# A two-block transformer kernel: the experts' gather by pairs in two bursts, and a first norm by a diagonal matrix

## The chip, the cores and the metric

The kernel runs on one core of one Trainium2 chip. The metric is the device time of one execution in microseconds. It is a single program of some 28,000 instructions on the engines TensorE (PE in the profile, its weight loads PEld), VectorE (DVE), ScalarE (ACT), GpSimd (POOL) and SyncE (SP, which here only issues transfers).

## The reference

The input x is 256 tokens of 1024 float32 values. Two blocks follow each other, and all arithmetic is float32. The chain is:

- a norm, a short convolution mixer, a norm, a dense SwiGLU (2816 wide);
- a norm, latent attention, a norm, a mixture of 8 experts (each a SwiGLU 2048 wide, two of them per token);
- SwiGLU, block attention, SwiGLU, SwiGLU, a state-space mixer (Mamba 2), SwiGLU, each with its norm.

Two parts matter here:

```python
def rmsnorm(x, g):
    xf = x.astype(jnp.float32)
    y = xf * lax.rsqrt(jnp.mean(xf * xf, axis=-1, keepdims=True) + EPS)
    return (y * g.astype(jnp.float32)).astype(x.dtype)

def moe_swiglu(h, router, w_gate, w_up, w_down):
    ...
    vals, idx = lax.top_k(probs, TOP_K)
    wts = vals / jnp.sum(vals, axis=-1, keepdims=True)
    ...
    for e in range(N_EXPERTS):
        out = out + gates[:, e:e + 1] * swiglu(ht, w_gate[e], w_up[e], w_down[e])
```

## The kernel before, in words

**Weights.** All large weights lie in HBM as slabs of 128 x 2048 float32 (1 MB). SP loads them in order into six buffers (`raw`); a load of slab s + 6 waits until slab s is split. ACT rounds a slab to the float32r format (`whi`, line 642, in `split_hi`), and DVE takes the rest (`wlo = raw - whi`, line 1142). There are three buffers for each of the two (`SPLIT`), so ACT begins slab n only when TensorE has used slab n - 3. Each product is three: hi by hi, hi by lo and lo by hi (`three`, lines 1874 to 1876, and `cols_slab`, lines 1949 to 1951). Activations are held as hi and lo parts in the same way.

**Order of work.** Every engine has one instruction stream in program order, and semaphores order them against each other. The code of each engine goes slab by slab: at slab k it first splits slab k + 2 (`ahead`) and then does what else stands at k.

**A norm that isn't deferred** is the first one and the one ahead of the state-space mixer. ACT squares and sums the two token tiles (`squares`, line 655), POOL computes the root (`root`, lines 515 and 517), DVE scales both tiles of x into `hn` (`scaled`, line 1170), and TensorE transposes `hn` in four banks' worth (`norm_T`, line 1901), with two buffers (`tp`) in turn. ACT (`norm_hi`, line 662) and DVE (`norm_lo`, line 1154) make the operand's hi and lo parts, multiplied by the gain, which is a column of `vecs`. Before the second of these norms TensorE runs 24 products with zeros (`idle_products`, line 1881), whose results nobody reads.

**The start.** Eleven small DMAs on ACT's queue load the gain and convolution vectors as rows into `vec_rows` (line 1082). TensorE runs 26 idle products, transposes the three row tiles (line 2578), DVE copies them to `vecs` (line 1803), and TensorE runs ten more idle products. SP waits for x before it issues the first slab.

**The experts** (`routed`). Where no expert has over 128 tokens, each expert's rows are gathered. Per expert there are 24 slabs in eight chunks of three: `up_a`, `up_b` (gate and up projections, k half by half) and `down`. After `up_b` come ACT's silu (line 745) and DVE's product (`h_tok`, line 1513); after `down` come TensorE's transposes of h_tok for the next chunk (line 2388), then `hT_hi` on ACT (line 752) and `hT_lo` on DVE (line 1517). `each_expert` writes out expert 0 and expert 7 and loops three times over a pair of an odd and an even one.

An expert's gather multiplies the token rows (`rows_hi`, `rows_lo`) by a 0/1 matrix `pick` of 256 tokens by 128 places. DVE makes `pick` (`choose`, line 1477) at slab 12; TensorE gathers after slab 14 in 32 products (line 2365) into two accumulator banks; ACT (line 728) and DVE (line 1486) convert the result to `xg_hi` and `xg_lo`, two of eight parts per slab, ACT at slabs 15 to 18 and DVE at 17 to 20. `pick` is transposed to `put` for the way back: ACT and DVE make `yg_hi` (line 735) and `yg_lo` (line 1495) at slab 2 of the next expert, TensorE scatters after slabs 3 and 5 (lines 2371 and 2372), and DVE adds to x at slabs 4 and 6 (line 1501). Ahead of expert 0 stand 22 idle products, its gather, and 12 idle products.

```python
                    if not last and k == OPERAND_AT - 1:
                        if not first:
                            pe.wait_ge(x_ready, f.x0 + 2 * ex)
                        gather(ex + 1, ex + 1)
```

Of the kernel before, what the change touches and what calls it, by code (L numbers as in the profile page):

```python
# [25 lines left out]
P = 128  # L26
# [25 lines left out]
OPERAND_AT = 15  # L52
# [5 lines left out]
def program(nc, a, out):  # L58
    ctx = ExitStack()
    with ctx:  # L60
# [67 lines left out]
        rows_loaded = sem("rows_loaded")  # L128
        rows_zero = sem("rows_zero")
        vecs_full = sem("vecs_full")  # L130
# [21 lines left out]
        def col(v, n):  # L152
            return vecs[:, v[0], v[1] + n:v[1] + n + 1]

        row_loads = [(V_MIX, 16, a["norm_mix"]), (V_FFN, 16, a["norm_ffn"]), (V_CONV, 24, a["conv_w"]),
                     (V_QA, 3, a["mla_q_a_norm"]), (V_KVA, 2, a["mla_kv_a_norm"]), (V_FFN1, 16, a["ffn1_norm_2"]),
                     (V_MIX2, 16, a["mix_norm_2"]), (V_FFN2, 16, a["ffn2_norm_2"]), (V_SCONV, 128, a["ssm_conv_w_2"]),
                     (V_SBIAS, 32, a["ssm_conv_b_2"]), (V_SNORM, 16, a["ssm_norm_2"])]

# [32 lines left out]
        vec_rows = big[:, 6144:6144 + 3 * P].rearrange("p (a b) -> p a b", a=3)  # L192
# [138 lines left out]

        rt = [area(8192 + 16 * n, 16).rearrange("p (t e) -> p t e", t=NT) for n in range(8)]
# [16 lines left out]
        pick = hT_hi[:, 2 * P:4 * P]  # L349
        put = big_r[:, 2 * D:2 * D + NT * P]  # L350
# [4 lines left out]
        yg_hi_done = sem("yg_hi_done")  # L355
        iota_i = area(8832, P).bitcast(I32)
# [99 lines left out]
        def each_expert(e, fn):  # L456

            def body(ex, first, last, parity):
                for k in range(0 if first else 2, 3 * (F_EXPERT // FC) + (0 if last else 2)):
                    fn(k, ex, first, last, parity)  # L460

            body(0, True, False, 0)
            with e.Fori(0, EXPERTS // 2 - 1) as i:
                body(2 * i + 1, False, False, 1)
                body(2 * i + 2, False, False, 0)
            body(EXPERTS - 1, False, True, 1)
# [12 lines left out]
        def _(sp):  # L479
# [16 lines left out]
            sp.wait_ge(x_loaded, 16 * NT)  # L496
# [138 lines left out]
        def _(act):  # L635
# [12 lines left out]
            def squares(f):  # L648
# [5 lines left out]
                for t in range(NT):  # L654
                    act.activation(hn[:, t], x[:, t], ACT.Square, accum_out=n_sum[:, f.m, t:t + 1]).then_inc(norm_sum, 1)

            def norm_hi(f, bs):
                v, g0 = f.gain
                for b in bs:
                    act.wait_ge(tp_full, f.u0 + b + 1)  # L660
                    for j in range(2):
                        r = act.activation(actA_hi[:, 2 * b + j, :], tp[:, (f.u0 + b) % 2, j * SEQ:(j + 1) * SEQ],
# [15 lines left out]
            def norm(f):  # L678
                if f.m == 0:
                    act.wait_ge(vecs_ready, 1)  # L680
# [39 lines left out]
            def routed(f):  # L720
# [3 lines left out]
                def operand(e, kt, parity):  # L724

                    if kt == 0:
# [1990 lines left out]
```

## Time and profile before

| | |
|---|---|
| time, median of 3 runs | 2200.74 us (2199.27 to 2201.12) |
| time of the profiled execution | 2198.36 us |
| its span in the profile | 2196.6 us |
| TensorE clock granted, mean | 0.989 |
| read from HBM | 454.77 MB, 208 GB/s over the span |

The experts take the stretch from about 450 to 1058 us of the span. In a timeline each row gives the start, the duration of the merged instructions, and in brackets the engine's idle time before them with what released it. A TensorE product's own duration is longer than the distance to the next one, because products overlap: the distance of the starts counts.

### The profile page before, as it was taken

How to read it: one execution, taken by the hardware profiler on the slowest of the kernel's cores; microseconds unless marked ns; L12 is line 12 of the kernel's file. 1: busy time of each engine (PE TensorE's matmuls, PEld its weight loads, DVE VectorE, ACT ScalarE, POOL GpSimd, SP SyncE). 2: the span in 40 equal slices, each digit the busy share in tenths (PEclk: the TensorE clock that was granted, in tenths of full speed). 3: DMA queues.
4: the chain of work that ended last, by engine and by line, in shares of the span. 5: the costliest groups of instructions: out<-in, count | busy, mean ns of one | idle time of the engine just before them, and what ended most of it. 6: DMA issues, size and time to landing. Idle time of an engine off the chain costs nothing.

```text
span 2196.6 us, 28406 instructions
## 1 busy us (share of the span) xinstructions
PE 2125.2 (97%) x10573; PEld 1777.1 (81%) x10573; DVE 1426.5 (65%) x1510; ACT 1182.0 (54%) x1361; POOL 56.6 (3%) x102
## 2 busy tenths in 40 slices
PE   9999998789999999999899999999999999989999
PEld 8888886578887888888788777888788799878887
DVE  5654556458889889889555585545555488585554
ACT  4444456357767777777444465444444466555433
POOL 1000001000000000000100010000000000000000
PEclk9999999989999999999999999999999999999999
DMA  8555433248898889889555443555455345314551
GB/s 278 182 182 191 166 141 115 78 180 339 329 360 326 344 326 357 328 344 355 183 186 191 158 168 125 199 184 185 172 187 191 138 154 193 133 41 180 185 188 57
DMA packets 64584, 457.07 MB, mean 208 GB/s; under 512 B 7457, under 2 KB 7950, under 8 KB 9838
## 3 DMA queue, kind: packets, MB, share of 16 engines
q1 hardware_dynamic: 63616, 455.24, 56.1%
q0 software_dynamic: 448, 0.46, 0.3%
q8 instruction: 59, 0.97, 0.2%
q14 instruction: 31, 0.25, 0.0%
q10 hardware_dynamic: 430, 0.15, 0.0%
HBM read 454.77 MB, written 1.05 MB: 208 GB/s over the span
## 4 chain that ended last, share of the span: by engine, by line
issue 63%; PE 30%; DVE 3%; POOL 1%; DVEq 1%; ACT 1%; ACTq 0%; POOLq 0%; DMA 0%
PE gu L1874 4%; PE gu L1876 4%; PE gu L1875 4%; PE acc L1874 3%; PE acc L1875 3%; PE acc L1876 3%; PE acc L1949 2%; PE acc L1951 2%; PE acc L1950 2%; DVE wlo L1142 1%; PE tp L1963 0%; PE tp L1901 0%; DVEq L1696 0%; POOL qk_rstd L612 0%; DVE big L1697 0%
## 5 line engine op out<-in xcount | busy, mean ns | idle before, releaser
L1142 DVE TENSOR_TENSOR wlo<-raw,whi 128x2048 fp32r<-128x2048 f32 (+1 forms) x436 | 989.5, 2271 | 417.1 <-ACT whi L642 415.9
L642 ACT ACTIVATE whi<-raw 128x2048 fp32r<-128x2048 f32 (+1 forms) x436 | 827.1, 1898 | 237.7 <-PE acc L1876 190.1
L1874 PE MATMUL gu<-whi,actA_hi 128*128 128x512 f32 (+1 forms) x1456 | 578.8, 398 | 2.7 <-DVE actA_lo L1154 1.8
L1876 PE MATMUL gu<-whi,actA_lo 128*128 128x512 f32 (+1 forms) x1456 | 567.7, 390 | 0.0
L1875 PE MATMUL gu<-wlo,actA_hi 128*128 128x512 f32 (+1 forms) x1456 | 566.4, 389 | 0.0
L1876 PEld LDWEIGHTS gu<-whi,actA_lo 128*128 128x128 f32 x1456 | 273.5, 188 | 58.5
L1874 PEld LDWEIGHTS gu<-whi,actA_hi 128*128 128x128 f32 x1456 | 274.0, 188 | 57.0 <-issue 3.9
L1875 PEld LDWEIGHTS gu<-wlo,actA_hi 128*128 128x128 f32 x1456 | 274.4, 188 | 53.0
L1874 PE MATMUL acc<-whi,hT_hi 128*128 128x512 f32 x656 | 257.3, 392 | 2.1 <-DVE hT_lo L1517 2.1
L1876 PE MATMUL acc<-whi,hT_lo 128*128 128x512 f32 x656 | 256.3, 391 | 0.0
L1875 PE MATMUL acc<-wlo,hT_hi 128*128 128x512 f32 x656 | 256.0, 390 | 0.0
L1874 PEld LDWEIGHTS acc<-whi,hT_hi 128*128 128x128 f32 x656 | 123.6, 188 | 30.8 <-DVE wlo L1142 2.6
L1876 PEld LDWEIGHTS acc<-whi,hT_lo 128*128 128x128 f32 x656 | 123.5, 188 | 26.0
L1875 PEld LDWEIGHTS acc<-wlo,hT_hi 128*128 128x128 f32 x656 | 123.6, 188 | 25.3
L695 ACT ACTIVATE hT_hi<-tp 128x512 fp32r<-128x512 f32 x50 | 29.9, 598 | 200.3 <-PE tp L1963 200.3
L1949 PE MATMUL acc<-actA_hi,whi 128*128 128x256 f32 x448 | 127.6, 285 | 0.8 <-DVE wlo L1142 0.8
L1951 PE MATMUL acc<-actA_hi,wlo 128*128 128x256 f32 x448 | 126.7, 283 | 0.0
L1950 PE MATMUL acc<-actA_lo,whi 128*128 128x256 f32 x448 | 126.7, 283 | 0.0
L1193 DVE TENSOR_TENSOR hT_lo<-tp,hT_hi 128x512 fp32r<-128x512 f32 x50 | 34.6, 692 | 115.6 <-ACT hT_hi L695 115.6
L1874 PE MATMUL acc<-whi,actA_hi 128*128 128x512 f32 (+1 forms) x224 | 89.1, 398 | 2.7 <-DVE actA_lo L1744 1.9
L710 ACT ACTIVATE silu_g<-gu,n_rstd 128x256 f32<-128x256 f32 x55 | 26.1, 475 | 119.3 <-PE gu L1876 119.3
L1949 PEld LDWEIGHTS acc<-actA_hi,whi 128*128 128x128 f32 x448 | 85.9, 192 | 1.1 <-DVE wlo L1142 1.1
(387 smaller groups left out, 2227.3 us busy)
## 6 DMA issues: line engine op xcount, KB each, us to landing
raw<-in_slabs SPq DMA_DIRECT2D x427, 1024.0 KB, 4.8
raw<-in_slabs SPq DMA_DIRECT2D x4, 576.0 KB, 3.8
raw<-in_slabs SPq DMA_DIRECT2D x2, 768.0 KB, 4.2
raw<-in_slabs SPq DMA_DIRECT2D x2, 640.0 KB, 3.9
x<-in_x SPq DMA_DIRECT2D x2, 512.0 KB, 3.8
out<-x SPq DMA_DIRECT2D x2, 512.0 KB, 2.8
raw<-in_slabs SPq DMA_DIRECT2D x1, 128.0 KB, 2.3
aux<-in_mla_q_norm POOLq DMA_DIRECT2D x1, 96.0 KB, 6.7
```

The costliest lines, as they stand in the source:

```text
L642: act.activation(whi[:, n0 % SPLIT, 0:w], raw[:, n0 % RAW, 0:w], ACT.Copy).then_inc(slab_hi, 1)
L695: act.activation(to[0], tp[:, (f.u0 + c) % 2], ACT.Copy).then_inc(tp_hi, 1)
L710: act.activation(silu_g[:, 1, :], gu[:, 1, 0:FC], ACT.Silu, scale=n_rstd[:, f.m - 1, 1:2]).then_inc(gu_silu, 1)
L1142: dve.tensor_tensor(wlo[:, n0 % SPLIT, 0:w], raw[:, n0 % RAW, 0:w], whi[:, n0 % SPLIT, 0:w].bitcast(F32), ALU.subtract).then_inc(slab_spli ...
L1193: dve.tensor_tensor(to[1], tp[:, (f.u0 + c) % 2], to[0].bitcast(F32), ALU.subtract).then_inc(tp_read, 1)
L1874: pe.matmul(o, xh, wh, start=start, stop=False)
L1875: pe.matmul(o, xh, wl, start=False, stop=False)
L1876: return pe.matmul(o, xl, wh, start=False, stop=stop)
L1949: pe.matmul(o, w[0][:, kt, bs], aT_hi[:, kt], start=kt == 0, stop=False)
L1950: pe.matmul(o, w[0][:, kt, bs], aT_lo[:, kt], start=False, stop=False)
L1951: r = pe.matmul(o, w[1][:, kt, bs], aT_hi[:, kt], start=False, stop=kt == KT - 1)
```

## The change

**The first norm and the one ahead of the state-space mixer.** ACT squares the first tile, DVE the second. POOL's root is as before. DVE then multiplies the identity by the root of each token (`rstd_diag`, two tiles of 128 x 128), and TensorE multiplies x by that diagonal matrix, which transposes and scales in one product, in float32. The very first norm uses four banks (two of them in `gu`) and doesn't wait for them to be read. The second of these norms has 18 idle products for 24.

**The vectors.** The host lays them out as columns, and one DMA on ACT's queue loads `vecs`. The row loads, the three transposes, the copy and ten of the idle products go; of the first 26 there remain 22. ACT runs a one-tile Square on zeros before it waits for x. SP issues slabs without a wait for x. On DVE slab 0's lo part now stands between the norm's first two banks and the last two.

**The experts.** Gathers are made for pairs (2q, 2q + 1). `pick` holds two experts' places side by side, in `hT_hi` for the first token tile and in `hT_lo` for the second. In an odd expert's slabs DVE chooses at slab 7; TensorE gathers half of the features after slab 8 and the other half after slab 15, with 16 products of 256 columns each, into the same two banks; ACT converts the even expert's part to `xg_hi` and copies the odd one's to `xg_odd` in float32, two of each per slab at 9 to 12 and 16 to 19; DVE makes the even expert's lo part, one of eight per slab, at 11 to 14 and 18 to 21. In an even expert ACT makes the odd one's `xg_hi` of `xg_odd` in one instruction at slab 12, and DVE its lo part at slab 13. The gather ahead of expert 0 is for the pair and uses four banks. `put` has two buffers, one per parity, and is made in chunk 1, not 3.

```diff
-OPERAND_AT = 15
+GATHER_AT = (8, 15)
+ODD_AT = 12
@@ norm, any engine
+        def norm_bank(f, b):
+            return gu[:, b - 2] if f.m == 0 and b >= 2 else tp[:, (f.u0 + b) % 2]
@@ SP
-            sp.wait_ge(x_loaded, 16 * NT)
@@ ACT, squares
-                for t in range(NT):
+                for t in range(NT if f.deferred else 1):
@@ ACT, routed
-                def operand(e, kt, parity):
-                    if kt == 0:
-                        act.wait_ge(gathered, e + 1)
-                    r = act.activation(xg_hi[parity][...], acc[:, 2 + kt // 4, ...], ACT.Copy, scale=col(v, g0 + kt))
+                def operand(q, kt, odd, base=2):
+                    if kt % 4 == 0 and not odd:
+                        act.wait_ge(gathered, 2 * q + kt // 4 + 1)
+                    o = xg_odd if odd else xg_hi[0]
+                    r = act.activation(o[:, kt * P:(kt + 1) * P], acc[in_pair(kt, odd, base)], ACT.Copy, scale=col(v, g0 + kt))
+                    if kt % 2 and odd:
                         r.then_inc(xg_hi_done, 1)
+                def odd_operand():
+                    act.drain()
+                    act.activation(xg_hi[1], xg_odd, ACT.Copy).then_inc(odd_hi_done, 1)
-                    if not last and OPERAND_AT <= k < OPERAND_AT + KT // 2:
-                        for j in range(2):
-                            operand(ex + 1, 2 * (k - OPERAND_AT) + j, 1 - parity)
+                    odd, q = pair
+                    if odd and not last:
+                        for n in range(2):
+                            if GATHER_AT[n] < k <= GATHER_AT[n] + 4:
+                                for j in range(2):
+                                    operand(q + 1, 4 * n + k - GATHER_AT[n] - 1, j)
+                    if not odd and k == ODD_AT:
+                        odd_operand()
@@ ACT, start
-            act.wait_ge(rows_zero, 1)
-            for v, n, src in row_loads:
-                ...
-                act.dma_start(vec_rows[...], ...).then_inc(rows_loaded, 16)
+            act.dma_start(vecs[:, :, :].rearrange("p a b -> p (a b)"), a["vecs"]).then_inc(vecs_ready, 16)
+            act.wait_ge(zero_ready, 1)
+            act.activation(area(2400, P), zero_r[:, :].bitcast(F32), ACT.Square)
@@ DVE, norm
-            def scaled(f):
-                dve.wait_ge(norm_rstd, f.m + 1)
-                for t in range(NT):
-                    dve.tensor_scalar(hn[:, t], x[:, t], n_rstd[:, f.m, t:t + 1], None, ALU.mult).then_inc(norm_tok, 1)
+            def diagonal(f):
+                if f.x0 == 0:
+                    dve.wait_ge(x_loaded, 16 * NT)
+                dve.drain()
+                dve.scalar_tensor_tensor(hn[:, 1], x[:, 1], 1.0, x[:, 1], ALU.mult, ALU.mult,
+                                         accum_out=n_sum[:, f.m, 1:2]).then_inc(norm_sum, 1)
+                dve.wait_ge(masks_ready, 2)
+                dve.wait_ge(norm_rstd, f.m + 1)
+                for t in range(NT):
+                    r = dve.tensor_scalar(rstd_diag[:, t], ident[:, :], n_rstd[:, f.m, t:t + 1], None, ALU.mult)
+                r.then_inc(norm_tok, 1)
@@ DVE, routed
+                        for odd in range(2):
+                            r = dve.tensor_scalar(pick[t][:, odd * P:(odd + 1) * P], iota, slot_of[:, at_expert(t, 2 * q + odd)],
+                                                  None, ALU.is_equal)
+                def odd_operand(q):
+                    dve.wait_ge(odd_hi_done, q + 1)
+                    dve.tensor_tensor(xg_lo[1], xg_odd, xg_hi[1].bitcast(F32), ALU.subtract).then_inc(odd_lo_done, 1)
-                    if not last and k == 12:
-                        choose(ex + 1)
+                    if odd and not last:
+                        if k == GATHER_AT[0] - 1:
+                            choose(q + 1)
+                        for n in range(2):
+                            if GATHER_AT[n] + 2 < k <= GATHER_AT[n] + 6:
+                                operand(q + 1, 4 * n + k - GATHER_AT[n] - 3)
+                    if not odd and k == ODD_AT + 1:
+                        odd_operand(q)
@@ DVE, start
-            dve.memset(vec_rows[:, :, :], 0.0).then_inc(rows_zero, 1)
-                scaled(stages_used[0])
-            dve.wait_ge(vecs_full, 1)
-            dve.tensor_copy(vecs[...], gu[:, 1, 0:3 * P]).then_inc(vecs_ready, 1)
-            ahead(0, -2)
-            norm(stages_used[0])
+                diagonal(stages_used[0])
+            norm_lo(stages_used[0], (0, 1))
+            ahead(0, -2)
+            norm_lo(stages_used[0], (2, 3))
@@ PE, norm
-                    if u >= 2:
+                    if u >= 2 and f.m:
                         pe.wait_ge(tp_read, u - 1)
-                            idle_products(gu[:, 0], 24)
-                        pe.wait_ge(norm_tok, 2 * (f.dm + 1))
+                            idle_products(gu[:, 0], 18)
+                        pe.wait_ge(norm_tok, f.dm + 1)
+                            if f.deferred:
+                                r = pe.transpose(o, part, ident[:, :])
+                            else:
+                                r = pe.matmul(o, part, rstd_diag[:, t], start=True, stop=True)
@@ PE, routed
-                def gather(e, n):
-                    pe.wait_ge(picked, n + 1)
-                    for kt in range(KT):
+                def gather(q, n, base=2):
+                    if n == 0:
+                        pe.wait_ge(picked, q + 1)
+                    elif base == 2:
+                        pe.wait_ge(xg_lo_done, 2 * q + 1)
+                    for kt in range(4 * n, 4 * n + 4):
-                    if kind == "up_a" and c % C == 0:
-                        pe.wait_ge(xg_lo_done, ex + 1 + c // C)
+                    if kind == "up_a" and c == C:
+                        if odd:
+                            pe.wait_ge(xg_lo_done, 2 * q + 4)
+                        else:
+                            pe.wait_ge(odd_lo_done, q + 1)
-                    if not last and k == OPERAND_AT - 1:
-                        if not first:
-                            pe.wait_ge(x_ready, f.x0 + 2 * ex)
-                        gather(ex + 1, ex + 1)
+                    if odd and not last and k in GATHER_AT:
+                        if k == GATHER_AT[0]:
+                            pe.wait_ge(x_ready, f.x0 + 2 * ex)
+                        gather(q + 1, GATHER_AT.index(k))
                 gather(0, 0)
+                gather(0, 1, 0)
@@ PE, start
-            idle_products(gu[:, 0], 26)
+            idle_products(gu[:, 0], 22)
             pe.wait_ge(masks_ready, 2)
-            pe.wait_ge(rows_loaded, 16 * len(row_loads))
-            for t in range(3):
-                r = pe.transpose(gu[:, 1, t * P:(t + 1) * P], vec_rows[:, t, :], ident[:, :])
-            r.then_inc(vecs_full, 1)
-            idle_products(gu[:, 0], 10)
-            pe.wait_ge(vecs_ready, 1)
```

## Rows read from the trace of the kernel before

**Rows 1.** The page, busy time of each engine over the span.

```profile
PE 2125.2 (97%) x10573; PEld 1777.1 (81%) x10573; DVE 1426.5 (65%) x1510; ACT 1182.0 (54%) x1361; POOL 56.6 (3%) x102
```

**Rows 2.** Windows in the experts: length, busy PE, PEld, DVE, ACT, POOL, clock, DMA, GB/s.

```profile
593.00:663.00 70.00, 69.73 (x329) 57.00 (x329) 61.79 (x51) 49.47 (x47) 0.00 (x0) 1.00 0.92 352
```

**Rows 3.** Waits from 457.4 to 1058 us: total, times, longest.

```profile
PEld tp L2388 <- DVE h_tok L1513: 8.1, 15, 2.8
```

**Rows 4.** Timeline of TensorE, transposes of h_tok in the second and third expert.

```profile
558.21 0.38 PE L2388 MATMUL tp<-ident,h_tok 128*128 128x128 f32 x2
...
566.63 0.38 PE L2388 MATMUL tp<-ident,h_tok 128*128 128x128 f32 x2
...
575.28 0.38 PE L2388 MATMUL tp<-ident,h_tok 128*128 128x128 f32 x2
...
587.34 0.38 PE L2388 MATMUL tp<-ident,h_tok 128*128 128x128 f32 x2
...
595.89 0.44 PE L2388 MATMUL tp<-ident,h_tok 128*128 128x128 f32 x2
...
604.71 0.44 PE L2388 MATMUL tp<-ident,h_tok 128*128 128x128 f32 x2
...
649.46 0.38 PE L2388 MATMUL tp<-ident,h_tok 128*128 128x128 f32 x2
```

**Rows 5.** Timeline of the start, 0 to 27 us, all engines.

```profile
1.12 7.86 PE L1881 MATMUL gu<-zero_r 128*128 128x512 f32 x26 [1.12 <-DVE zero_r L1135]
...
5.46 37.67 SPq L483 DMA_DIRECT2D raw<-in_slabs  x12
...
6.49 1.28 ACT L655 ACT_TABLE_LOAD   x1 [6.49 <-issue]
...
10.40 0.72 POOL L517 TENSOR_TENSOR n_rstd<-n_ms,n_half 128x2 f32<-128x2 f32 x1
...
12.95 2.28 DVE L1142 TENSOR_TENSOR wlo<-raw,whi 128x2048 fp32r<-128x2048 f32 x1
...
15.61 1.04 PE L1901 MATMUL tp<-ident,big 128*128 128x128 f32 x8
...
19.31 0.36 PE L1949 MATMUL acc<-actA_hi,whi 128*128 128x256 f32 x1
...
22.26 0.28 PE L1949 MATMUL acc<-actA_hi,whi 128*128 128x256 f32 x1
```

**Rows 6.** Windows of the start, columns as in rows 2.

```profile
3.00:4.00 1.00, 1.00 (x4) 0.81 (x3) 0.00 (x0) 0.00 (x0) 0.00 (x0) 1.00 1.01 406
...
12.20:14.00 1.80, 1.80 (x5) 1.36 (x5) 1.80 (x3) 0.18 (x1) 1.80 (x4) 0.50 1.02 432
```

**Rows 7.** Timeline of DVE in the second expert.

```profile
560.19 0.42 DVE L1517 TENSOR_TENSOR hT_lo<-tp,hT_hi 128x256 fp32r<-128x256 f32 x1
...
574.53 0.47 DVE L1477 TENSOR_SCALAR hT_hi<-big 128x128 fp32r<-128x128 f32 x2
```

**Rows 8.** Timeline of ACT in the second expert.

```profile
572.81 0.39 ACT L745 ACTIVATE silu_g<-gu 128x256 f32<-128x256 f32 x1 [0.86 <-PE gu L1876]
573.10 1.92 ACT L642 ACTIVATE whi<-raw 128x2048 fp32r<-128x2048 f32 x1
```

**Rows 9.** Timeline of the norm ahead of the state-space mixer.

```profile
1745.66 1.04 ACT L655 ACTIVATE big<-x 128x1024 f32<-128x1024 f32 x1
...
1747.96 1.50 DVE L1170 TENSOR_SCALAR big<-x,n_rstd 128x1024 f32<-128x1024 f32 x2 [3.38 <-POOL n_rstd L517]
...
1749.51 1.09 PE L1901 MATMUL tp<-ident,big 128*128 128x128 f32 x8 [0.82 <-DVE big L1170]
```

**Rows 10.** Timeline of TensorE in the state-space mixer.

```profile
1902.02 1.05 PE L2518 MATMUL acc<-h_tok 128*128 128x128 f32 x8
...
1905.38 0.65 PE L2533 MATMUL gu<-aux 128*128 128x256 f32 x2
```

**Rows 11.** Groups by line, the gathers' products with rows_lo.

```profile
L2365 PE MATMUL acc<-hT_hi,actB_lo 128*128 128x128 f32 x128 | 29.0, 276 | 0.0
```

More of the change, by code:

```diff
@@ L348, in program @@
         yg_hi, yg_lo = [big_r[:, D * n:D * n + D] for n in range(2)]
-        pick = hT_hi[:, 2 * P:4 * P]
-        put = big_r[:, 2 * D:2 * D + NT * P]
+        pick = [v[:, 2 * P:4 * P] for v in (hT_hi, hT_lo)]
+        xg_odd = area(3072, D)
+        put = [big_r[:, 2 * D + NT * P * n:2 * D + NT * P * (n + 1)] for n in range(2)]
         route_const, route_sel, route_cum, route_flag, rows_hi_done, rows_lo_done = [sem(n) for n in (
@@ L749, in at @@
                         bank = tp[:, (f.u0 + t) % 2]
-                        if t == 3:
-                            act.activation(put, bank[:, 2 * P:4 * P], ACT.Copy)
+                        if t == 1:
+                            act.activation(put[pair[0]], bank[:, 2 * P:4 * P], ACT.Copy)
                         act.activation(hT_hi[:, 0:2 * P], bank[:, 0:2 * P], ACT.Copy).then_inc(tp_hi, 1)
-                    if not last and OPERAND_AT <= k < OPERAND_AT + KT // 2:
-                        for j in range(2):
-                            operand(ex + 1, 2 * (k - OPERAND_AT) + j, 1 - parity)
+                    odd, q = pair
[6 more added lines that the diff above has]
+                        odd_operand()
                 for kt in range(KT):
-                    operand(0, kt, 0)
+                    for j in range(2):
+                        operand(0, kt, j, (2, 0)[kt // 4])
                 each_expert(act, at)
@@ L1502, in add, with at @@
                                              x[:, t], ALU.mult, ALU.add).then_inc(x_ready, 1)
-                def at(k, ex, first, last, parity):
+                def at(k, ex, first, last, pair):
                     kind, c = ffn_kind(f, k, ex)
@@ L1518, in at @@
                                           ALU.subtract).then_inc(tp_read, 1)
-                    if not last and k == 12:
-                        choose(ex + 1)
-                    if not last and OPERAND_AT + 2 <= k < OPERAND_AT + 2 + KT // 2:
-                        for j in range(2):
-                            operand(ex + 1, 2 * (k - OPERAND_AT - 2) + j, 1 - parity)
+                    odd, q = pair
+                    if odd and not last:
[6 more added lines that the diff above has]
+                        odd_operand(q)
                 choose(0)
                 for kt in range(KT):
-                    operand(0, kt, 0)
+                    operand(0, kt, (2, 0)[kt // 4])
                 each_expert(dve, at)
@@ L2706 @@
     weights = slabs({k: np.asarray(v) for k, v in inputs.items() if k in PACKED})
[L2707 to L2708 removed]
+    plain = {k: v for k, v in inputs.items() if k not in PACKED | COLUMNS}
+    for name, value in {**plain, "slabs": weights, "vecs": columns(inputs), **constants()}.items():
         v = np.ascontiguousarray(value)
```

109 lines of the change are left out of this document (54 added, 55 removed).

## The prediction

> **What bounds the kernel now.** I read the page first: TensorE is busy for 97% of the span [rows 1], so only what shortens TensorE's own queue, or a wait in front of it, can move the time. Then the experts' stretch by windows: in a typical 70 us PE is busy for 69.7, DVE for 61.8, ACT for 49.5, and the DMA engines carry 352 GB/s at a 0.92 share [rows 2]. PE sets the pace; DVE has little left. Then the waits of that stretch, of which the transposes' wait for DVE's h_tok, 8.1 us in 15 times, is one of TensorE's longest [rows 3]; no engine waits there for a weight transfer. Last the timeline of the transposes, which come once per three slabs and so act as a ruler [rows 4]: 558.21 to 566.63 is 8.42 us for three slabs with nothing between; the next gap is 8.65 (two transposes of `pick` in it); the one with the gather is 12.06; the two after it are 8.55 and 8.82, for DVE then has two operand conversions at each slab. A gather in the loop so costs 3.64 + 0.13 + 0.40 = 4.17 us. Seven of the eight gathers are in the loop: **29.2 us**. From 8.42, with some 0.25 for the transposes, a slab is 2.72.
>
> **The first norm.** Before, ACT issues eleven DMAs and reaches its table load at 6.49; squares, root and scaling follow; n_rstd is ready at 11.12, ten idle products stand before the transposes at 15.61, slab 0 is split at 15.23, and its first matmul runs at 19.31 [rows 5]. After, one DMA replaces the eleven on ACT's queue, the table load moves in front of the wait for x, SP doesn't wait for x (its first slab was issued at 5.46) and DVE takes one of the squares. In order: 0.2 MB of vectors beside x at 406 GB/s [rows 6] puts x at 5.9 for 5.4; squares to 7.2 (DVE's is unseen; the split's 2.28 for 2048 elements makes it about half of that, 1.15 to 1.3); POOL's root 1.1 (0.72 is the power) to 8.35; two diagonals of 128 columns, 0.47 as the picks of [rows 7], to 8.85. The 22 idle products (26 took 7.86) end by 8.1 and cost nothing. Sixteen products into four banks end near 10.8. Meanwhile slab 0 follows x and the vectors: 5.9 + 1.05 MB at 406 GB/s = 8.5. ACT: whi, 1.92 by [rows 8], to 10.4, then eight norm_hi of 0.39, as that group's other row, to 13.6; DVE: norm_lo of two banks, 0.42 each half as in [rows 7], to 12.9, wlo of slab 0 to 15.2. That is the new start, 4.0 us earlier. But PE now stands idle from 10.8 to 15.2, and before, idle from 8.98 on was followed by a granted clock of 0.50, the 1.2 GHz level, in 12.2 to 14.0 [rows 6]. If the low clock holds for twice that stretch, the 256-column products of slab 0 take some 0.21 instead of 0.12 each (24 in 2.95 us, [rows 5]): 1.6 lost. I take **2.4**, between 0.5 (vectors and slabs delay x by two more) and 4.2 (the clock stays up). Slab 1 is split near 19.2, before slab 0 is used up. POOL's own DMAs stay behind its root and only come earlier. Four banks save the waits for tp_read, but DVE is what ends last here.
>
> **The norm before the state-space mixer.** ACT's second square (1.04 at 1745.66) goes to DVE beside the first, where it ends 0.2 later; two scalings (1.50 at 1747.96) become two diagonals of 0.47. So the transposes now at 1749.51 come 1.04 - 0.2 + 1.03 = 1.9 earlier [rows 9]. Six idle products fewer are 6 x 2.72 / 12 = 1.4; PE stood idle for 0.82 in front of the transposes, so 0.3 of that is left and nothing is held up. What follows (hi, lo, two banks) moves along. The products with the diagonal are true f32 matmuls. Such a product of 128 columns has a pitch of (1.05 - 0.27) / 7 = 0.11 us, one of 256 columns about 0.24 [rows 10], and the present transposes have 0.11 too (eight in 1.04, [rows 5]): no price. I take **1.8**, between 0.5 (the clock falls in another place) and 2.2. The Trainium skill (TensorE: Matmul & The Clock Gate, Terms) says that transpose mode is 4x faster for FP32, so that leaving it should cost; at 128 columns this trace disagrees, and what the rule would make of the time is the third rival's.
>
> **The experts.** Each gather of today is 32 products of 128 columns ([rows 11]: 128 of the half rows_lo, as many of the other), 3.64 us in the ruler, 0.114 each. A pair's gather is 32 products of 256 columns, 0.123 each by slab 0 [rows 5], 3.9 us, in two bursts: twice the columns cost nearly the same. The gather ahead of the loop grows by 0.3 and has sixteen conversions on ACT for eight, in the shadow of twelve idle products; if that cover were short it is 0.3 to 0.5 once. In the loop three pair gathers, 11.7, replace 29.2: at most 17.5 saved. New waits:
> - The choice is of four, 0.94, twice the 0.47 of [rows 7], and stands at slab 7, one slab before the burst. In the body shown, DVE's hT_lo starts at 560.19, so the picks are ready at 561.5; slab 8 ends at 566.63 - 2 x 2.72 = 561.2. PE waits **0.4**, and behind it stand the burst's results and slab 9; DVE's next split is 0.6 late, for which the burst itself makes room. Three times.
> - DVE's operand conversions are one per slab over eight slabs, not two over four, with a burst before each four: **0.2** for today's 0.53.
> - The odd half of a pair: in each even expert ACT copies 128x1024 at slab 12 and DVE subtracts at 13. Read against the body shown: silu at 572.81, whi of slab 15 at 573.10 for 1.92 [rows 8]. With a copy (half a whi, 1.0) between them whi ends at 576.0 and wlo at 578.25, just when PE needs it (575.28 + 0.25 + 2.72). hT_lo and the subtraction (1.15, half a split) put wlo of slab 16 at 579.75 to 582.0, and PE wants it at 581.0: **1.0** late, four times.
> So 3 x (3.9 + 0.4 + 0.2) + 4 x 1.0 = 17.5 stands against 29.2: **11.7** saved. Ends: 17.5 (no new wait) and 7.4 (waits of 1.5 a pair, copies 1.2 each: 16.2 + 5.6 with the conversions' own). The transposes of `pick` stay two per expert; the scatter is untouched.
>
> **The sum.** 2.4 + 1.8 + 11.7 = 15.9. The profiled execution took 2198.36 us, which gives 2182.5; the median of the runs shown, 2200.74, is 2.4 above it, and against that the forecast is **2184.8**.
>
> **Rivals.**
> 1. The odd copies and picks hide after all, and PE pays for little but the products. For it: DVE's adds of 128x1024 at slabs 4 and 6 leave no mark on the ruler at 566.63. Against: there the scatter gives PE other work. Experts 17.0, sum 21.2: 2179.5. Chance 0.14.
> 2. More conflict, the lower end: 7.4 + 4.2 = 11.6: 2189.1. Chance 0.08.
> 3. Products with the diagonal run at four times the transposes' pitch, 0.44. The second bank of the first norm is then full at 12.4, slab 0 is split at 16.3 (1.1 lost), and the later norm, whose four banks cost 1.3 more each, partly side by side, loses 3.5: 2189.4. This is what the skill's sentence on transpose mode would make. Against it stands the 0.11 of [rows 10]. Chance 0.05.
> 4. Transfers bind the experts. 575.28 to 649.46 is one expert [rows 4], 24 slabs of 1.05 MB in 74.2 us, 339 GB/s. If 340 were the most, the experts would gain nothing: sum 4.2, about 2196. Against: no wait for raw, and 352 in [rows 2], where the forecast asks for 346. Chance 0.06.
> 5. **Slower.** DVE becomes the pace at the burst slabs: the choice, the lo halves that the second burst waits for, and the odd subtraction each come behind a split that went first, one slab late. Ten places (3 + 3 + 4). Without new waits the sum is 21.7; above 2.2 us a place the change loses, above 2.6 it loses more than can be mistaken, and at a whole slab, 2.72, the time is 2206. For: DVE 61.8 of 70. Against: two conversions per slab cost 0.53 in all. Chance 0.03.
> That the experts take the all-token branch, so that the change is void there, is excluded for this input by the products of [rows 11].
>
> **The numbers.** Forecast 0.64, rivals 0.14, 0.08, 0.05, 0.06, 0.03. The range joins the bounds of the terms: 0.5 + 0.5 + 7.4 = 8.4 to 4.2 + 2.2 + 17.5 = 23.9 saved, 2176.8 to 2192.3; it leaves out rivals 4 and 5. What a measurement of this kernel can tell from no change is 0.2%, 4.4 us. Faster by more: all but rival 5 and half of rival 4, 0.94; within 0.2% 0.03; slower 0.03.
>
> **What would show it.** Start: n_rstd near 8.3, the first matmul of slab 0 near 15.2, with half-clock products after it; a start near 17 would mean that x or slab 0 came late. Later norm: transposes about 1.0 behind n_rstd's own end with a pitch of 0.11. Experts: the ruler should read 8.4 and 1.9 more in a gap with a burst, 0.4 more at the first; about 9.4 once in each even expert, where the odd half is subtracted; two experts that took 148.4 should take about 145.5. ACT waiting for raw, or gaps over 10.8 without a scatter, would prove me wrong.

## The result, and the profile after

| | before | after |
|---|---|---|
| median of the runs | 2200.01 us (4 runs) | 2182.36 us (4 runs) |
| lowest to highest | 2197.30 to 2201.12 | 2180.46 to 2186.71 |
| profiled execution | 2198.36 | 2180.46 |
| its span | 2196.6 | 2178.7 |
| TensorE busy | 2125.2, 10573 instructions | 2104.8, 10454 |

The ratio is 0.9931, with an interval of 0.9915 to 0.9947: 15.2 us faster (11.7 to 18.7), where 15.9 was forecast. The two medians of the table lie 17.7 apart, inside the same interval. The two profiled spans differ by 17.9 us. TensorE stays the bound. This is the page's line of busy times after, to be set against [rows 1]:

```profile
PE 2104.8 (97%) x10454; PEld 1760.3 (81%) x10454; DVE 1422.8 (65%) x1484; ACT 1184.7 (54%) x1362; POOL 56.0 (3%) x102
```

TensorE is 20.4 us less busy, DVE and ACT are what they were. Five points of TensorE's timeline split the 17.9 us of the two spans:

| point | before | after | gained up to it |
|---|---|---|---|
| first product of slab 0 | 19.31 | 15.54 | 3.8 |
| first product of the gather ahead of expert 0 | 450.35 | 446.75 | 3.6 |
| last transposes in the experts | 1046.22 | 1030.46 | 15.8 |
| idle products ahead of the state-space mixer | 1743.09 | 1727.35 | 15.7 |
| first full-width product of that mixer | 1757.39 | 1739.55 | 17.8 |

So 3.6 us came at the start, 12.1 in the experts and 2.1 in the later norm. Nothing was given back between. Not all of it is the change's: at three of these places the profile of before has TensorE at a low clock where another execution of the same code has it high, and that is 1.7 us at the start, 1.6 at expert 0 and 1.3 in the later norm (experiment 2 and the hardware section). Without these 4.6 the 17.9 would be 13.3.

**The start.** The timeline of all engines after, 0 to 30 us, to be read against [rows 5]:

```profile
1.11 6.68 PE L1905 MATMUL gu<-zero_r 128*128 128x512 f32 x22 [1.11 <-DVE zero_r L1143]
...
1.24 1.28 ACT L1090 ACT_TABLE_LOAD   x1 [1.24 <-PEq L2749]
...
6.30 1.06 ACT L653 ACTIVATE big<-x 128x1024 f32<-128x1024 f32 x1 [3.45 <-DMA x<-in_x]
...
6.36 1.23 DVE L1180 SCALAR_TENSOR_TENSOR big<-x 128x1024 f32<-128x1024 f32 x1 [5.29 <-DMA x<-in_x]
...
8.02 0.71 POOL L515 TENSOR_TENSOR n_rstd<-n_ms,n_half 128x2 f32<-128x2 f32 x1
...
9.48 2.02 PE L1929 MATMUL tp<-silu_g,x 128*128 128x128 f32 x16 [1.68 <-DVE silu_g L1185]
...
11.34 1.95 PE L1929 MATMUL gu<-silu_g,x 128*128 128x128 f32 x16
...
13.20 2.28 DVE L1150 TENSOR_TENSOR wlo<-raw,whi 128x2048 fp32r<-128x2048 f32 x1
...
15.54 0.39 PE L1976 MATMUL acc<-actA_hi,whi 128*128 128x256 f32 x1 [2.25 <-DVE wlo L1150]
```

The table load lies in the wait for x, x is worked on at 6.30, and the root is ready at 8.73 (11.12 before). The last waits end in the order forecast: DVE's part of the split of slab 0 (`wlo`) releases TensorE. The two rows of line 1929 say something that the prediction had not read: two banks are eight products, and the row counts 16. A true float32 product of 128 columns leaves two records, where a transpose leaves one (eight per two banks in [rows 5]).

**The experts.** The ruler after, TensorE's transposes of h_tok, through most of an odd expert and all of the even one behind it ([rows 4] before):

```profile
540.74 0.38 PE L2418 MATMUL tp<-ident,h_tok 128*128 128x128 f32 x2
...
550.30 0.38 PE L2418 MATMUL tp<-ident,h_tok 128*128 128x128 f32 x2
...
561.00 0.38 PE L2418 MATMUL tp<-ident,h_tok 128*128 128x128 f32 x2
...
569.43 0.38 PE L2418 MATMUL tp<-ident,h_tok 128*128 128x128 f32 x2
...
579.86 0.38 PE L2418 MATMUL tp<-ident,h_tok 128*128 128x128 f32 x2
...
605.31 0.38 PE L2418 MATMUL tp<-ident,h_tok 128*128 128x128 f32 x2
...
615.19 0.38 PE L2418 MATMUL tp<-ident,h_tok 128*128 128x128 f32 x2
...
624.75 0.38 PE L2418 MATMUL tp<-ident,h_tok 128*128 128x128 f32 x2
...
641.58 0.38 PE L2418 MATMUL tp<-ident,h_tok 128*128 128x128 f32 x2
...
651.43 0.38 PE L2418 MATMUL tp<-ident,h_tok 128*128 128x128 f32 x2
```

A plain gap (561.00 to 569.43) is 8.43. The gaps of 9.88 and 9.56 hold the scatter, as in every expert, the second now with the transposes of `pick` too. What the change put in:

- 550.30 to 561.00, 10.70: the first burst, 1.92 for its 16 products and 0.36 of waiting.
- 569.43 to 579.86, 10.43: the second burst, 1.92 and 0.09.
- 641.58 to 651.43, 9.85: the odd half of a pair in an even expert, 1.43.

The waits of the stretch 440 to 1040 us (total, times, longest), against [rows 3]:

```profile
PEld tp L2418 <- DVE h_tok L1535: 2.8, 1, 2.8
...
PEld acc L2395 <- DVE hT_lo L1494: 1.5, 3, 0.5
```

TensorE waits once for h_tok, 15 times before. New are three waits of 0.5 for the picks, one ahead of each first burst.

The gap of 12.06 of [rows 4] is gone. From 540.74 one odd and one even expert take 146.1 us (the row one loop later is at 686.83); the prediction wanted 145.5 in place of 148.4.

### The profile page after: what moved, and what is told of

Same layout as the page of the kernel before. It is cut to its first block, busy times and chain, and to the rows that moved or that the text cites. A ratio compares the mean times of both kernels' runs of the same rounds, so it can differ in the third digit from the quotient of the medians.

```text
span 2178.7 us, 28140 instructions
## 1 busy us (share of the span) xinstructions
PE 2104.8 (97%) x10454; PEld 1760.3 (81%) x10454; DVE 1422.8 (65%) x1484; ACT 1184.7 (54%) x1362; POOL 56.0 (3%) x102
## 3 DMA queue, kind: packets, MB, share of 16 engines
HBM read 454.82 MB, written 1.05 MB: 209 GB/s over the span
## 4 chain that ended last, share of the span: by engine, by line
issue 63%; PE 30%; DVE 3%; POOL 1%; DVEq 1%; ACT 1%; DMA 0%; POOLq 0%; ACTq 0%; SPq 0%
PE gu L1898 4%; PE gu L1900 4%; PE gu L1899 4%; PE acc L1898 3%; PE acc L1899 3%; PE acc L1900 3%; PE acc L1976 2%; PE acc L1978 2%; PE acc L1977 2%; DVE wlo L1150 1%; PE tp L1990 0%; DVEq L1722 0%; POOL qk_rstd L610 0%; DMA raw<-in_slabs 0%; ACT whi L640 0%
```

## The experiments

The line numbers of kernel.py differ a little from kernel to kernel. All ratios are against the kernel before, which ran beside each.

**1. The norms alone.** The change's hunks of the start, the vectors and the two norms; the experts as before.

```diff
+            act.dma_start(vecs[:, :, :].rearrange("p a b -> p (a b)"), a["vecs"]).then_inc(vecs_ready, 16)
-                scaled(stages_used[0])
+                diagonal(stages_used[0])
...
```

> The change's norms and vectors alone, with the experts as before. If the parts add up, this saves what the trace of the changed kernel shows outside the experts: 3.8 us at the start and 2.1 us at the later norm, 5.9 us together, ratio 0.9973; slab 0's first product starts at 15.5 us, and the three-slab gaps of the experts read 12.05, 8.55 and 8.82 us after each gather as before. Rival: most of the start's gain is granted clock that another execution need not give; then slab 0's products have a pitch of 0.21 us in this run and the saving is 3 to 4 us.

Measured: 2195.68, ratio 0.9985 (0.9975 to 0.9994), 3.3 us and so less than expected (1.3 to 5.5 by the interval). Its profiled execution shows the same steps as the changed kernel: slab 0 begins at 15.67, the mixer's first full-width product stands 12.24 behind the idle products (14.30 before, 12.20 after), and its span, 2190.5, is 6.1 shorter. So the profiled execution gained what the pair of profiles said, and the median less. That made TensorE's clock suspect.

**2. The experts alone.** The change's hunks of `routed`; start and norms as before.

```diff
-                    if not last and k == OPERAND_AT - 1:
...
-                        gather(ex + 1, ex + 1)
+                    if odd and not last and k in GATHER_AT:
...
+                        gather(q + 1, GATHER_AT.index(k))
...
```

> The pair gather alone, with norms and vectors as before. The ruler of the changed kernel gives 29.4 us before and 13.4 (three pair gathers with their waits) plus 5.7 (four odd halves) after, so 10.3 us saved if expert 0's first three slabs run at the low clock as before, 11.9 if they do not: ratio 0.9953 or 0.9946. Rival (transfers or DVE give part of it back elsewhere in this stretch): under 8 us.

Measured: 2187.12, ratio 0.9947 (0.9931 to 0.9964), 11.7 us. The ruler takes 568.74 us from first to last transposes (580.67 before, 568.58 after); 1.6 of that difference is the clock at expert 0, whose first three slabs take 8.47 here and after, and 10.04 before. The parts add up, 3.3 + 11.7 = 15.0 against 15.2: the start is not paid for in the experts, nor the other way. This kernel has the start of before, instruction for instruction, and still begins slab 0 at 17.61, not 19.31. TensorE's timeline of it from 10 us:

```profile
11.52 2.56 PE L1908 MATMUL gu<-zero_r 128*128 128x512 f32 x10
...
17.61 0.36 PE L1976 MATMUL acc<-actA_hi,whi 128*128 128x256 f32 x1
```

Before, the same ten idle products took 4.00 at 11.77. The window 11.30 to 15.60 (columns as in [rows 2]) of before, and then of this kernel:

```profile
11.30:15.60 4.30, 4.24 (x13) 3.42 (x14) 3.93 (x4) 1.08 (x1) 4.30 (x7) 0.60 1.19 408
```

```profile
11.30:15.60 4.30, 3.65 (x21) 2.93 (x21) 4.03 (x5) 1.86 (x4) 4.30 (x7) 1.00 1.16 398
```

A granted clock of 0.60 against 1.00, with the same code ahead of it. The start of before is worth 19.3 in one execution and 17.6 in another, so of the 3.8 us that the start shows in the pair of profiles 1.7 depends on which execution of before was taken.

**3. The odd half in four pieces.** One copy and one subtraction of 128 x 1024 in an even expert become four of 128 x 256, two slabs apart.

```diff
-ODD_AT = 12
+ODD_AT = (9, 11, 13, 15)
-                    if not odd and k == ODD_AT + 1:
-                        odd_operand(q)
+                    if not odd and k - 1 in ODD_AT:
+                        odd_operand(q, ODD_AT.index(k - 1))
```

> The changed kernel, with the odd half made in four pieces of 256 columns: ACT at slabs 9, 11, 13, 15, DVE at 10, 12, 14, 16. If the 1.4 us that each even expert loses comes from two lumps in a row (a copy of 1.0 on ACT that makes slab 15's split late, a subtraction of 1.2 on DVE that makes slab 16's late), the 9.85 us gap falls to 8.5 and four of them save 5.3 us on the changed kernel. Rival: DVE as such lacks the time in this stretch, whatever the cut; then the loss spreads over other gaps and under 2 us is saved.

Measured: 2176.4, ratio 0.9905 (0.9886 to 0.9924). Its ruler in the same even expert:

```profile
643.07 0.38 PE L2422 MATMUL tp<-ident,h_tok 128*128 128x128 f32 x2
...
651.48 0.38 PE L2422 MATMUL tp<-ident,h_tok 128*128 128x128 f32 x2
```

The gap of 9.85 is 8.41. The odd half costs 1.4 us four times where it comes in one piece; the same work in four pieces costs nothing. (The cut and the slabs at which the work stands were changed together; a single piece was tried at one other slab only, in experiment 8.) The timeline of the changed kernel says who is late, ACT and DVE from 639 us:

```profile
639.57 1.06 ACT L734 ACTIVATE actA_hi<-big 128x1024 fp32r<-128x1024 f32 x1
...
640.54 1.90 ACT L640 ACTIVATE whi<-raw 128x2048 fp32r<-128x2048 f32 x1
...
642.47 2.29 DVE L1150 TENSOR_TENSOR wlo<-raw,whi 128x2048 fp32r<-128x2048 f32 x1 [1.56 <-ACT whi L640]
...
644.82 0.19 PEld L1898 LDWEIGHTS gu<-whi,actA_hi 128*128 128x128 f32 x1 [0.54 <-DVE wlo L1150]
...
645.01 1.21 DVE L1512 TENSOR_TENSOR actA_lo<-big,actA_hi 128x1024 fp32r<-128x1024 f32 x1
...
646.15 4.48 DVE L1150 TENSOR_TENSOR wlo<-raw,whi 128x2048 fp32r<-128x2048 f32 x2
...
648.56 0.49 PE L1898 MATMUL acc<-whi,hT_hi 128*128 128x512 f32 x1 [0.72 <-DVE wlo L1150]
```

ACT's copy holds back `whi` by 1.06; DVE waits 1.56 for it, and its `wlo` reaches TensorE 0.5 late. Then DVE's 1.21 makes the next `wlo` late by the rest, some 0.9. The prediction had the second of these and called the first just in time.

**4. The choice two slabs earlier.**

```diff
-                        if k == GATHER_AT[0] - 1:
+                        if k == GATHER_AT[0] - 3:
```

> The changed kernel, with DVE's choice two slabs earlier, at slab 5. If TensorE's wait in front of the first burst (0.36 us, three times) is only the place of the choice, the 10.7 us gap falls to 10.35 and 1.1 us is saved. Rival: at slab 5 the choice lies between DVE's two additions of 1.28 us and makes a split late; then the gaps with the scatter (9.56) grow by up to 0.5 us each and nothing is saved.

Measured: 2182.58, ratio 0.9929 (0.9908 to 0.9950), what the change has. Most of the wait ahead of the first burst goes, and as much comes back one gap earlier. The ruler of that odd expert:

```profile
544.57 0.38 PE L2418 MATMUL tp<-ident,h_tok 128*128 128x128 f32 x2
...
554.55 0.44 PE L2418 MATMUL tp<-ident,h_tok 128*128 128x128 f32 x2 [0.27 <-DVE h_tok L1535]
...
564.97 0.38 PE L2418 MATMUL tp<-ident,h_tok 128*128 128x128 f32 x2
```

9.98 and 10.42 where the change has 9.56 and 10.70: 0.28 off one, 0.42 onto the other. Slab 5 lies between DVE's two additions of the scatter, at slabs 4 and 6 (1.28 us each), and 0.94 more makes h_tok late.

**5. Pieces, and the choice ahead of slab 7's split.** Experiment 3, with `choose` moved in front of `ahead` in the same slab, so that the picks do not queue behind a split of 2.28.

```diff
+                    if pair[0] and not last and k == GATHER_AT[0] - 1:
+                        choose(pair[1] + 1)
                     ahead(f.s0, k, 0, C // 2 * ex)
```

> The odd half in four pieces as in the experiment before, and DVE's choice at slab 7 ahead of that slab's split and not behind it. If the wait in front of the first burst is only an order on DVE's queue, the burst itself hides the split that is now later: the 10.7 us gap falls to 10.35, the gap with the scatter stays 9.56 (at slab 5 it grew to 9.98), and the kernel is 1.1 us under the one with the pieces alone, some 6.5 under the changed kernel: about 2175 us, ratio 0.9895. Rival: the split that is 0.95 late reaches slab 9 or 10 and another gap grows by as much.

Measured: 2177.42, ratio 0.9900 (0.9883 to 0.9916). The first burst's gap is 10.36 and the one ahead of it stays 9.56; the whole ruler 563.64 (564.62 in experiment 3). That is 1.0 us in the trace and nothing that the medians can tell from experiment 3.

**6. With idle products in two gaps.** By now TensorE's clock was the suspect in two places: at slab 0, behind a wait of 2.25 us (2.52 in experiment 5), and at expert 0's first transposes, behind one of 2.34. Experiment 5, with eight idle products behind those of the first norm and nine ahead of expert 0's first transposes:

```diff
+                    if f.m == 0 and b == 3:
+                        idle_products(acc[:, 3], 8)
...
                         if k == 1:
+                            idle_products(gu[:, 1], 9)
                             transposes(0, ex, odd)
```

> The same with idle products in two gaps of TensorE: eight behind the first norm's products, nine before the first transposes of expert 0 (where it waits 2.34 us). If the 1.6 us in expert 0's first three slabs (10.07 or 8.47) and the 1.5 us in slab 0 (21 or 33 products in 15.5 to 19.5 us) are both the granted clock after an idle stretch, both always read the fast value here, and the median lies 0.5 to 3 us under the kernel without them, with less spread. Rival: the clock falls for another reason; then either slow value can still show, and the products only add what they take beyond the gap (none).

Measured: 2173.49, ratio 0.9889 (0.9872 to 0.9905). In its trace slab 0 runs at a clock of 1.00, and expert 0's first three slabs take 8.49 where experiment 5 took 10.10. The median is 3.9 us under experiment 5's; 0.5 to 3 were expected.

**7. Transposes for the diagonal products.** It leaves out the scaling by the root in the two norms; DVE still makes the diagonals.

```diff
-                                r = pe.matmul(o, part, rstd_diag[:, t], start=True, stop=True)
+                                r = pe.transpose(o, part, ident[:, :])
```

> The changed kernel with plain transposes of x by the identity where it multiplies by the diagonal; left out is the scaling by the root in those two norms. If a true float32 product costs two passes (0.23 us) and a transpose one (0.11), the first norm's sixteen end at 11.4 and not 13.3, slab 0 still starts at 15.5 because ACT and DVE end last, and TensorE idles for 4.1 us in front of it; by the theory that the gap decides, the clock is low in slab 0 (21 products in 15.5 to 19.5 us) and the time is 1.5 us longer there. The later norm gets 0.9 to 1.3 us shorter (first product of the mixer 11 us after the idle products' start, not 12.2). Rival (a true product costs what a transpose does, as the prediction had it): nothing moves in either norm.

Measured: 2179.59, ratio 0.9913 (0.9897 to 0.9930). TensorE's timeline of the start:

```profile
9.67 1.06 PE L1929 MATMUL tp<-ident,x 128*128 128x128 f32 x8 [1.44 <-DVE silu_g L1185]
10.57 1.04 PE L1929 MATMUL gu<-ident,x 128*128 128x128 f32 x8
15.57 0.58 PE L1976 MATMUL acc<-actA_hi,whi 128*128 128x256 f32 x1 [3.96 <-DVE wlo L1150]
```

Sixteen products take some 1.9 us in place of 3.8, sixteen records in place of thirty-two. A true float32 product of 128 columns so leaves two records and takes 0.23 us, a transpose one and 0.12. The start doesn't care, 15.57 for 15.54: the idle time grows to 3.96, and slab 0 then runs at the low clock. The later norm does care, for there the banks wait for each other: +11.08 from the idle products to the first full-width product in place of +12.20, 1.1 us. The timeline of that norm in the changed kernel:

```profile
1731.94 2.05 PE L1929 MATMUL tp<-silu_g,x 128*128 128x128 f32 x16 [0.34 <-DVE silu_g L1185]
...
1734.93 2.05 PE L1929 MATMUL tp<-silu_g,x 128*128 128x128 f32 x16 [0.95 <-DVE actA_lo L1162]
...
1739.55 0.28 PE L1976 MATMUL acc<-actA_hi,whi 128*128 128x256 f32 x1
```

**8. The odd half's subtraction one slab later.** The changed kernel, in one execution only, so that its trace is read here and not its time.

```diff
-                    if not odd and k == ODD_AT + 1:
+                    if not odd and k == ODD_AT + 2:
```

> The changed kernel with only DVE's subtraction of the odd half moved from slab 13 to 14; ACT's copy stays at 12. Two lumps in a row (my reading): ACT's copy alone makes slab 15 0.5 late, the subtraction's 0.9 goes, and the 9.85 us gap reads about 8.9. Rival (the subtraction alone is the cost, ACT's copy hides): it reads 8.45. Rival (only the sum counts): 9.85 as before, or split over two gaps.

Measured: 2186.04. The gaps with the odd half in the ruler, and the late instructions between them:

```profile
647.95 0.38 PE L2418 MATMUL tp<-ident,h_tok 128*128 128x128 f32 x2
...
653.59 1.22 DVE L1512 TENSOR_TENSOR actA_lo<-big,actA_hi 128x1024 fp32r<-128x1024 f32 x1
...
656.93 0.42 DVE L1535 TENSOR_TENSOR h_tok<-gu,silu_g 128x256 f32<-128x256 f32 x1
...
657.40 0.44 PE L2418 MATMUL tp<-ident,h_tok 128*128 128x128 f32 x2 [0.47 <-DVE h_tok L1535]
```

The gap is 9.45, not the 8.9 expected: the 0.5 of ACT's copy stays, and the subtraction now makes h_tok 0.47 late. The loss falls from 1.43 to 1.03 and the next gap grows by up to 0.1. At both slabs tried, 13 and 14, some of DVE's 1.2 us in one piece shows.

**9, 10, 11. The two fills on the changed kernel, the changed kernel again, and experiment 6's again**, side by side, to price the clock with everything else equal. Experiment 9's edit is the diff of experiment 6, on the changed kernel; the other two have none.

> The changed kernel with only the two fills (eight idle products behind the first norm's products, nine before expert 0's first transposes). If the gap decides the clock, slab 0 has 33 products in 15.5 to 19.5 us and expert 0's first three slabs take 8.47 us, and the median is 1 to 3 us under the changed kernel's in the same chip's runs (1.5 + 1.6 times the share of executions in which the clock would have fallen). Rival: the fast values of the last run with fills were luck; one of the two reads slow here, and the medians agree.

> The changed kernel again, unchanged, as the partner of the run before. Both gaps are there (2.3 us each), so each of the two places may read fast or slow (slab 0: 33 or 21 products; first three slabs: 8.47 or 10.07). Ratio to before 0.9925 to 0.994. Rival (the first profile's fast values belong to the change): both read fast again.

> The best kernel again: odd half in four pieces, the choice ahead of the split, both fills. Slab 0 and expert 0 fast again, 8.41 to 8.44 in each even expert where 9.85 stood, 10.36 at the first burst; 6.5 us under the run with the fills alone. Rival: one of the two places is slow in spite of its fill.

| kernel | median (lowest to highest) | ratio (interval) | ruler |
|---|---|---|---|
| the change with fills (9) | 2178.43 (2176.99 to 2181.44) | 0.9914 (0.9900 to 0.9928) | 568.63 |
| the change again (10) | 2183.72 (2183.23 to 2184.80) | 0.9935 (0.9922 to 0.9949) | 570.22 |
| pieces, choice, fills again (11) | 2172.64 (2172.05 to 2176.67) | 0.9889 (0.9872 to 0.9906) | 561.97 |

The window of slab 0, 15.5 to 19.5 us (columns as in [rows 2]), in the changed kernel's first and second profile:

```profile
15.50:19.50 4.00, 3.96 (x33) 3.96 (x34) 4.00 (x6) 2.27 (x2) 0.00 (x0) 1.00 0.93 297
```

```profile
15.50:19.50 4.00, 3.95 (x22) 3.96 (x23) 4.00 (x6) 2.27 (x2) 0.00 (x0) 0.63 0.99 318
```

Then of the change with fills:

```profile
15.50:19.50 4.00, 3.91 (x32) 3.91 (x33) 4.00 (x7) 2.32 (x2) 0.00 (x0) 1.00 0.95 315
```

One kernel, the same 2.25 us of waiting ahead of slab 0, and 33 products in 4 us in one execution, 22 in the other. Expert 0's first transposes in the changed kernel's second profile, and then with the fill:

```profile
463.60 0.65 PE L2418 MATMUL tp<-ident,h_tok 128*128 128x128 f32 x2 [2.34 <-DVE h_tok L1535]
...
473.64 0.38 PE L2418 MATMUL tp<-ident,h_tok 128*128 128x128 f32 x2
```

```profile
456.71 2.20 PE L1905 MATMUL gu<-zero_r 128*128 128x512 f32 x9
...
459.22 0.44 PE L2420 MATMUL tp<-ident,h_tok 128*128 128x128 f32 x2 [0.30 <-DVE h_tok L1535]
...
467.69 0.38 PE L2420 MATMUL tp<-ident,h_tok 128*128 128x128 f32 x2
```

10.04 falls to 8.47, 1.6 us; slab 0 gives 1.5. Together 3.1, where the medians differ by 5.3 (1 to 3 were expected). From slab 0's first product to the gather's it is 428.5 us with fills and 432.9 without in this pair. That holds slab 0's 1.5 and 2.9 more, in code that no kernel here changes, and the 2.9 falls in the last 30 us ahead of the gather, most of it at its 22 idle products. TensorE's timeline there with fills, and then without:

```profile
436.62 7.63 PE L1905 MATMUL gu<-zero_r 128*128 128x512 f32 x22 [6.20 <-issue]
```

```profile
438.51 1.65 PE L1905 MATMUL gu<-zero_r 128*128 128x512 f32 x3 [6.57 <-issue]
442.01 6.62 PE L1905 MATMUL gu<-zero_r 128*128 128x512 f32 x19 [1.85 <-issue]
```

From the first idle product to the gather it is 7.47 us with fills and 9.96 without, and 1.85 of the difference is a pause behind the third of them, for which the profile shows no cause. Nine of the thirteen profiles have such a pause, of 1.3 to 2.7 us; the three with fills and experiment 7 have none. The fills stand elsewhere, so whether they have a part in that is not shown, and why the pause comes is open. Over all profiles the stretch from slab 0 to the gather lies between 428.5 and 436.3 (431.0 before, 431.2 after).

## Why the prediction was right, and where not

The forecast time, 2184.8, is 2.4 above the median of the change's first runs and 1.1 above that of experiment 10. The chances went to the right side, and the forecast's own case came, not a rival. By its steps:

- **The bound** was read rightly: TensorE's queue and DVE's waits in the experts.
- **The experts, 11.7: measured 10.4, the mechanism as put.** The ruler took 580.67 us before and 570.22 in experiment 10, both with expert 0 at the low clock. (Expert 0's first three slabs are 10.04 there too; in the first profile after they were 8.47, which is the 1.6 that makes 12.1 of 10.4.) A pair's gather, 3.9 forecast, is 3.84 by the 0.12 of its products. The pick wait, 0.4, is 0.36. Conversions and the wait of the second burst, 0.2, are 0.28.
- **The odd half, 1.0 four times, was the term mis-sized: 1.36 to 1.45 each**, 5.7 in all for 4.0. The step that failed is "wlo at 578.25, just when PE needs it": the chain of ACT's copy, `whi` and `wlo` came out half a microsecond past the need, and the subtraction in DVE's order then added the 0.9 that had been priced. A sum that lands "just in time" has an error of its own; it should have gone into the term as a wait of 0 to 0.5.
- **The start, 2.4: 1.9 to 2.1 at the same clock.** The chain was right step by step: table load hidden, x at 6.30 for 5.9, root at 8.73 for 8.35, first product at 15.54 for 15.2. But the sum set it against 19.31, and the same start of before also gives 17.61 (experiment 2), from which the change's 15.54 and experiment 1's 15.67 are 2.1 and 1.9 away. Up to the gather the two profiles of the changed kernel show 3.6 and 1.9, with all that the clock and the pause there add. The loss of 1.6 to a low clock in slab 0 did not show in the first profile after and did in experiments 3, 5, 8 and 10, with the same code up to there: right in size, and wrong to be a single case. That 2.4 is so near comes in part by luck, for the 1.6 taken off happens to offset the 1.7 by which before's start was slow in its profile. The wait of 4.4 given as the reason came only in experiment 7 (3.96); in the change the sixteen products end near 13.3, not 10.8, and leave 2.25.
- **The later norm, 1.8: 2.1 in the pair of profiles, 0.8 at the same clock.** Its transposes begin 1.83 earlier behind the idle products, as the step said (1.9), but the products with the diagonal take 1.1 of that back (experiment 7). The other 1.3 is before's clock: its window there stands at 0.72, and experiment 2, with that code unchanged, takes 12.97 instead of 14.30. So the term was 1.0 too large, by the next step, and that 2.1 stands near 1.8 is luck.
- **"No price" for the products with the diagonal is the step that was wrong.** It rested on [rows 10], eight records of true float32 products in 1.05. Those eight records are four products. Such a product costs 2 times a transpose, 0.12 us more each. At the start it is hidden behind DVE (experiment 7, 15.57 for 15.54); in the later norm it costs 1.1 us. The Trainium skill (TensorE: Matmul & The Clock Gate, Terms) has transpose mode 4x faster for FP32; at 128 columns the runs show 2x, which agrees in direction and not in size. (A float32r product of 128 columns takes 0.114 us here as well, so a transpose that is faster in itself might not show at this size.) The third rival took the 4x, and its 3.5 us loss is more than three times what came.
- **Rival 1** (all hides): the odd half in pieces does hide, in experiment 3, but not in one piece. **Rival 2**, the lower end: its waits of 1.5 a pair didn't come (none is over 0.5), but its 1.2 for an odd half was passed, by 0.2. **Rival 4**: transfers bind nothing; with pieces and fills the experts run still faster on the same slabs. **Rival 5**: DVE's order costs 0.1 to 1.4 at its places, under the 2.2 from which it would have decided.

**The ledger against the median.** It counts 1.9 or 3.6 at the start, 10.4 or 12.1 in the experts, 0.8 or 2.1 in the later norm, by the clocks that these profiles had: 13.1 to 17.8. The lower end is the change at equal clocks, some 2.8 under the 15.9 forecast: 0.5 at the start, 1.3 in the experts (odd halves 1.7 worse, the rest 0.4 better) and 1.0 in the later norm. The measured 15.2 and, in experiment 10, 14.3 lie in it. Experiment 1's 3.3 is near what its trace gains over the start and the later norm of experiment 2 (17.61 - 15.67 = 1.9, and 12.97 - 12.24 = 0.7), and its 6.1 is the gain over the profile of before; how often each clock comes in the runs that were only timed can't be seen, so that this is how the 3.3 comes about was argued, not shown.

**A better version** follows from the two corrections. Odd halves in pieces (5.6 us in the ruler of experiment 3, net of expert 0's clock), the choice ahead of the split (1.0) and idle products in two gaps give 2173.49 and, again, 2172.64, both times at a ratio of 0.9889: some 24.4 us under the kernel before (0.0111 of 2200), where the change alone has 14 to 15.

## What to carry to other kernels

When TensorE is the bound, put a periodic instruction's start times side by side: the gap that grew names the slab, and the engine whose release stands there names the price. An operand conversion of half a slab that went into this tight pipeline in one piece cost 1.4 of the 2.3 us that its two instructions take; cut into four, two slabs apart, it cost nothing. Before taking a product's duration from a row, count products in the code against records in the row.

## What the runs showed of the hardware

- **Float32 products.** A true float32 product of 128 columns is two records of 0.12 us, 0.23 together; a transpose of the same size is one, 0.12. Of float32r, 128 columns cost 0.114 and 256 cost 0.12: twice the columns for 5% more, which is the whole gain of the pair gathers.
- **The clock after a wait of 2.3 us is not fixed by the code.** At slab 0, behind 2.25 us of waiting (2.52 in experiment 5), the clock was 1.00 in the changed kernel's first profile and in experiments 1 and 4, and 0.57 to 0.63 in experiments 3, 5, 8 and 10. At expert 0, behind 2.34, it was high after and in experiments 2 and 7, and low (10.04 to 10.10 for 8.47) before and in experiments 1, 3, 4, 5, 8 and 10. Each low case runs at the 1.2 GHz level for a while and costs 1.5 to 1.6 us. The executions differ before the wait already: the start's 22 idle products, the same code in all, took 6.68, 6.84 and 8.13 us in the three high cases and 7.07 to 7.70 in the four low ones. With 8 and 9 idle products in the two gaps the clock was high in both, in experiments 6, 9 and 11.
- **Two profiles of the same code differ by this alone.** Before's own start cost 1.7 more in its profile than in experiment 2's. A pair of profiles can so show a gain of a few microseconds that the medians do not have.
- **A pause without a shown cause.** Ahead of expert 0 TensorE stops for 1.3 to 2.7 us within 22 idle products in nine of thirteen profiles (1.85 in experiment 10's), and not in the other four.
